# A second batch's preparation and end in another order, and the last expert tile of a MoE kept in SBUF

## The reference, cut to what matters

```python
def _rwkv7(r, k, v, xw, xa, xg, ...):            # 8 heads of 64
    logw = -softplus(-(w0 + tanh(xw) @ w_up)) - 0.5
    decay = exp(-exp(logw))
    a = sigmoid(a0 + xa @ a_up)
    kk = normalized(heads(k * k_k))
    k_mod = k * (1.0 + (a - 1.0) * k_a)
    y = _rwkv7_scan(r, decay, k_mod, v, kk, kk * a)
    yn = (y - mean(y)) * rsqrt(var(y) + GN_EPS) ...
    return (yn + bonus * v) * g

def hierarchical_moe(h, ...):                    # 16 experts, 2 per token
    weights, expert_idx = router(h)
    u = silu(hf @ w_gate[e]) * (hf @ w_up[e]) * combine
    return einsum("nef,efd->nd", u, w_down)
# afterwards: rmsnorm(x + moe, norm_final_g)
```

## Time and profile before

| | us |
|---|---|
| median of 3 runs (lowest to highest) | 1575.68 (1571.98 to 1575.98) |
| the profiled execution | 1576.64 |
| its span in the profile | 1574.4 |
| PE busy | 1473.1 (94%) |
| DVE, ACT, POOL busy | 739.1, 604.9, 464.0 |
| chain that ended last, PE's share | 83% |

### The profile page before, as it was taken

How to read it: one execution, slowest core, us unless ns; L and a number is a source line. 1 busy time by engine, 2 the same in 40 slices (tenths; PEclk the granted TensorE clock), 3 DMA queues, 4 the chain that set the end, 5 groups by cost and what they waited for, 6 DMA issues and landing times.

```text
span 1574.4 us, 19313 instructions
## 1 busy us (share of the span) xinstructions
PE 1473.1 (94%) x7736; PEld 1154.6 (73%) x7736; DVE 739.1 (47%) x1156; ACT 604.9 (38%) x948; POOL 464.0 (29%) x162
## 2 busy tenths in 40 slices
PE   6999997899879999999998999999999988699995
PEld 5878876688668888888876887666687867577762
DVE  3356277733353532515132596334352335566663
ACT  4443245322353332323134124533333444255552
POOL 2352122000225664646423444320134520200002
PEclk9999998657899999999998999999999999799998
DMA  6232112000135445354432333200123521889964
GB/s 209 87 121 68 56 66 95 2 1 1 46 129 160 135 146 159 124 158 142 139 107 80 98 112 99 80 27 27 49 85 107 188 58 67 346 314 422 419 261 188
DMA packets 97803, 203.90 MB, mean 130 GB/s; under 512 B 6672, under 2 KB 56208, under 8 KB 91056
## 3 DMA queue, kind: packets, MB, share of 16 engines
q1 hardware_dynamic: 90656, 176.94, 32.6%
q10 hardware_dynamic: 4752, 17.30, 2.7%
q0 software_dynamic: 2304, 8.39, 1.4%
HBM read 168.54 MB, written 34.08 MB: 129 GB/s over the span
## 4 chain that ended last, share of the span: by engine, by line
PE 83%; DVE 6%; ACT 5%; issue 3%; DMA 2%; POOL 1%; SPq 0%; POOLq 0%; DVEq 0%; ACTq 0%
PE bank L517 21%; PE bank L499 12%; PE bank L501 12%; PE bank L500 12%; PE bank L2770 4%; PE bank L780 3%; PE bank L799 3%; PE bank L790 2%; PE bank L1193 2%; PE bank L782 1%; ACT whi L428 1%; PE bank L706 1%; PE bank L2716 1%; PE bank L1149 1%; PE bank L1252 1%
## 5 line engine op out<-in xcount | busy, mean ns | idle before, releaser
L436 POOL TENSOR_TENSOR wlo<-raw,whi 128x2048 fp32r<-128x2048 f32 (+2 forms) x83 | 378.7, 4562 | 698.1 <-ACT whi L428 672.0
L428 ACT ACTIVATE whi<-raw 128x2048 fp32r<-128x2048 f32 (+1 forms) x84 | 159.1, 1894 | 279.6 <-PE bank L501 272.1
L517 PE MATMUL bank<-alo,whi 128*128 128x512 f32 x368 | 149.5, 406 | 4.9 <-DVE alo L728 4.9
L1986 DVE TENSOR_TENSOR ffn_relu<-ffn_relu 128x512 f32<-128x512 f32 x32 | 97.7, 3052 | 107.0 <-ACT ffn_relu L1966 107.0
L517 PE MATMUL bank<-ahi,whi 128*128 128x512 f32 x368 | 146.5, 398 | 0.0
L499 PE MATMUL bank<-alo,whi 128*128 128x512 f32 (+1 forms) x360 | 141.1, 392 | 0.0
L501 PE MATMUL bank<-ahi,wlo 128*128 128x512 f32 (+1 forms) x360 | 140.3, 390 | 0.0
L500 PE MATMUL bank<-ahi,whi 128*128 128x512 f32 (+1 forms) x360 | 140.1, 389 | 0.0
L517 PE MATMUL bank<-ahi,wlo 128*128 128x512 f32 x368 | 91.7, 391 | 0.0
L517 PEld LDWEIGHTS bank<-alo,whi 128*128 128x128 f32 x368 | 71.3, 194 | 23.5 <-DVE alo L728 6.1
L517 PEld LDWEIGHTS bank<-ahi,whi 128*128 128x128 f32 x368 | 71.4, 194 | 15.5 <-issue 0.7
(11 more groups left out here) (483 smaller groups left out, 3005.2 us busy)
## 6 DMA issues: line engine op xcount, KB each, us to landing
raw<-in_w_in_dram SPq DMA_DIRECT2D x18, 1024.0 KB, 5.1
expert_gate_up<-in_expert_w_gate_dram SPq DMA_DIRECT2D x17, 1024.0 KB, 11.8
expert_gate_up<-in_expert_w_up_dram SPq DMA_DIRECT2D x17, 1024.0 KB, 14.2
expert_down<-in_expert_w_down_dram SPq DMA_DIRECT2D x17, 1024.0 KB, 9.2
raw<-in_w_ffn_up_dram SPq DMA_DIRECT2D x16, 1024.0 KB, 6.2
raw<-in_w_ffn_down_dram SPq DMA_DIRECT2D x16, 1024.0 KB, 5.6
raw<-in_w_in_first_dram SPq DMA_DIRECT2D x12, 1024.0 KB, 5.5
expert_rows_dram<-zero_rows SPq DMA_DIRECT2D x23, 512.0 KB, 6.9
```

The costliest lines, as they stand in the source:

```text
L428: nc.scalar.activation(whi[:, n % SPLIT, 0:k * c], raw[:, n % RAW, 0:k * c], ACT.Copy).then_inc(hi_made, 1)
L436: nc.gpsimd.tensor_tensor(wlo[:, n % SPLIT, 0:k * c], raw[:, n % RAW, 0:k * c], whi[:, n % SPLIT, 0:k * c].bitcast(F32), ALU.subtract).the ...
L517: ins = nc.tensor.matmul(acc, of, by, start=first and i == 0, stop=last and i == products - 1)
L1986: nc.vector.tensor_tensor(relu2[:, n % 2, :], relu[:, n % 2, :], relu[:, n % 2, :], ALU.mult).then_inc(up_sq, 1)
```

## The change

Three places change. In the second batch, `FILL_LAST` is rewritten, rr1 and rv1/0 stay ahead of `over_norm` and rv1/1 comes behind it; `wlo` and `alo` move behind the preparation (`AFTER_PREP`); the product kk * aaa * e_inv is made as kk * (aaa * e_inv), so POOL needs e_inv and no longer kk; the end has another order. In the MoE, tile 16's result stays in SBUF and is added by PE with a selection matrix (`kept_w`, made from `kept_picks`), so that the gathers wait for tiles 14 and 15 only; down(15) stands ahead of the second half of gate_up(16); the order of the sums is changed. The branches for further tiles are nested, and their number is loaded early.

```diff
+        AFTER_PREP = 4
-        FILL_LAST = [0, 6, 6, 0, 3, 1, 1, 1, 1, 1, 1] + [1] * INVERT_PARTS + [2, 2, 2, 2, 2, 2, 2, 2, 2, 3, 3, 3, 3, 2, 2]
+        FILL_LAST = [0, 6, 3, 0, 3, 4, 1, 1, 1, 1, 1] + [1] * INVERT_PARTS + [2, 1, 1, 2, 2, 2, 2, 2, 1, 3, 3, 3, 2, 3, 5]
...
                 if made:
                     st.after("dve", made)
+                else:
+                    pe.wait_ge(z_shifted, 1 + [unit for unit, *_ in z_units].index(f"rv{p // 2}/{p % 2}"))
...
-            st.after("pool", "ka")
-            st.done(tt(b.beta[:, :], b.ka, b.e_inv, ALU.mult), "beta")
+            st.after("pool", "ae")
             st.after("dve", "kk")
+            st.done(tt(b.beta[:, :], b.kk, b.ae, ALU.mult), "beta")
...
         def pool_fill_last(pool):
-            yield from range(2 * WIDE_STEPS - 1)
+            yield from range(4 * WIDE_STEPS + AFTER_PREP)
             make_lo(pool, pool_slab, slab_no["rr1"] + 1 + SPLIT)
-            yield
-            yield from range(2 * WIDE_STEPS - 1)
             for p in (0, 1):
                 pool_rw_lo(pool, p)
             yield
...
-            st.after("dve", "kk")
-            st.done(tt(b.ka, b.kk, b.aaa, ALU.mult), "ka")
+            st.after("act", "e_inv")
+            st.done(tt(b.ae, b.aaa, b.e_inv, ALU.mult), "ae")
...
+        KEPT = SURE - 1
+        def tiles_beyond(eng, used, tile, i=SURE):
+
+            if i < MOE_TILES:
+                with eng.If(used > i - NE):
+                    tile(i)
+                    tiles_beyond(eng, used, tile, i + 1)
...
+            turn_hidden(pe, KEPT - 1)
+            pe_gate_up(pe, KEPT, 0)
+            pe_down(pe, KEPT - 1)
+            pe_gate_up(pe, KEPT, 1)
+            pe_sum_start(pe)
+            turn_hidden(pe, KEPT)
+            pe_down(pe, KEPT)
+            tiles_beyond(pe, used, lambda i: pe_later(pe, i))
             pe_sum(pe)
...
+            for t in SUM_ORDER:
...
+                nc.tensor.matmul(LEFT_BANKS[t][:, :], kept_w[:, t, :], y_rows[:, KEPT % 2, LEFT], start=t == IN_SBUF, stop=t == IN_SBUF,
+                                 skip_group_check=True)
+                nc.tensor.matmul(RIGHT_BANKS[t][:, :], kept_w[:, t, :], y_rows[:, KEPT % 2, RIGHT], start=True, stop=True).then_inc(halves_summed, 1)
...
+            in_order("rows rows kept rows kept rows kept final kept final final final",
+                     rows=dve_sum(dve, steps), kept=dve_sum_kept(dve, steps), final=dve_final(dve, steps))
...
-            for i in range(SURE - 2, SURE):
-                tile_done(pool, y_stored, i, 16)
+            for i in range(KEPT - 2, KEPT):
+                pool.wait_ge(*y_stored_at(i))
```

More of the change, by code:

```diff
@@ L886, in wk @@
                 return work[:, n:n + m, :].rearrange("p a n -> p (a n)")
-            b.cum, b.cumx, b.e_in, b.e_inv, b.e_ex, b.aaa, b.knorm, b.kk, b.kmod, b.ka, b.rk, b.sig = (wk(n) for n in range(12))
+            b.cum, b.cumx, b.e_in, b.e_inv, b.e_ex, b.aaa, b.knorm, b.kk, b.kmod, b.ae, b.rk, b.sig = (wk(n) for n in range(12))
             b.kr = put(f"rw_kr{s}", [P, NCH, 2, CHUNK])
@@ L1711, in pool_fill_last @@
             yield
-            yield from range(NHEAD * NT + 4 + TURN_ROUNDS - 1)
+            yield from range(NHEAD * NT + 4 + TURN_ROUNDS - 2 - AFTER_PREP)
             pool.wait_ge(rows_normed, turns["attn1"]["tile"] + NT)
@@ L2728, in pick_rows, with turn_kept_picks @@
                 ins.then_inc(rows_turned[0], 1)
+        def turn_kept_picks(pe):
+            pe.wait_ge(picks_made, 3 + 2 * NT + TOPK * NT)
+            for t in range(NT):
+                for k in range(TOPK):
+                    ins = nc.tensor.matmul(HIDDEN_BANKS[0][:, t * P:(t + 1) * P], kept_picks[:, k, t, :], ident,
+                                           start=k == 0, stop=k == TOPK - 1, skip_group_check=True)
+            ins.then_inc(halves_summed, 1)
         def pe_first_gate_up(pe):
@@ L2788, in pe_phase5 @@
             pe_first_gate_up(pe)
+            turn_kept_picks(pe)
+            used = later_tiles_used(pe)
             turn_rows(pe, 1)
-            for i in range(1, SURE):
+            for i in range(1, KEPT):
                 pe_gate_up(pe, i, 0)
+                if i == 1:
+                    pe.wait_ge(route_exps, 3)
                 turn_hidden(pe, i - 1)
@@ new lines, in pe_phase5, with pe_later @@
+            pe_gate_up(pe, KEPT, 0)
[5 more added lines that the diff above has]
+            tiles_beyond(pe, used, lambda i: pe_later(pe, i))
+            pe_sum(pe)
+        def pe_later(pe, i):
+            turn_rows(pe, i)
+            for c in range(CHUNKS):
+                pe_gate_up(pe, i, c)
+            turn_hidden(pe, i)
+            pe_down(pe, i)
+            tile_done(pe, y_left, i)
+            tile_done(pe, y_right, i)
+            pe_sum_start(pe)
@@ L2877, in act_phase5 @@
             act_tile_in(act, 3)
+            act.wait_ge(halves_summed, 1)
+            nc.scalar.activation(kept_w[:, :, :], four(HIDDEN_BANKS[0]), ACT.Copy).then_inc(route_exps, 1)
             for i in range(1, SURE):
@@ L3042, in dve_phase5 @@
                     steps.link(nc.vector.tensor_scalar(diag_w[:, k, t, :], ident, weight[:, k, t:t + 1], None, ALU.mult))
+            steps.link(nc.vector.tensor_scalar(kept_slot[:, :, :], slot_f[:, :, :], float(-KEPT * P), None, ALU.add))
+            for k in range(TOPK):
+                for t in range(NT):
+                    nc.vector.tensor_scalar(kept_picks[:, k, t, :], slot_no, kept_slot[:, k, t:t + 1], weight[:, k, t:t + 1],
+                                            ALU.is_equal, ALU.mult).then_inc(picks_made, 1)
             dve.wait_ge(rows_issued, 1)
@@ L3067, in dve_phase5, with dve_later @@
-            in_turn(dve_sum(dve), later(2, dve_final(dve, steps)))
-        def dve_sum(dve):
+            dve_y(dve, KEPT)
+            tiles_beyond(dve, used, lambda i: dve_later(dve, i))
+            in_order("rows rows kept rows kept rows kept final kept final final final",
+                     rows=dve_sum(dve, steps), kept=dve_sum_kept(dve, steps), final=dve_final(dve, steps))
+        def dve_later(dve, i):
+            for c in range(CHUNKS):
+                dve_w_lo(dve, i, c)
+            dve_x_lo(dve, i)
+            dve_hidden(dve, i)
+            dve_y(dve, i)
@@ L3078, in dve_sum, with dve_sum_kept @@
+        def dve_sum_kept(dve, steps):
+            for t in SUM_ORDER:
+                dve.wait_ge(halves_summed, KEPT_SUMMED[t])
+                if t == IN_SBUF:
+                    steps.link(nc.vector.tensor_tensor(x[:, t, LEFT], x[:, t, LEFT], LEFT_BANKS[t][:, :], ALU.add))
+                nc.vector.tensor_tensor(x[:, t, RIGHT], x[:, t, RIGHT], RIGHT_BANKS[t][:, :], ALU.add).then_inc(y_sums, 1)
                 yield
@@ L3163, in sp_phase5 @@
             sp_later(sp, NE)
-            for i in range(SURE, MOE_TILES):
-                with sp.If(used > i - NE):
-                    sp_later(sp, i)
+            tiles_beyond(sp, used, lambda i: sp_later(sp, i))
             out_view = out[0].rearrange("(t p) d -> p t d", p=P)
-            for t in range(NT):
-                sp.wait_ge(final_rows, 2 * t + 2)
+            for n, t in enumerate(SUM_ORDER):
+                sp.wait_ge(final_rows, 2 * n + 2)
                 sp.dma_start(out_view[:, t, :], out_rows[:, t, :]).then_inc(out_stored, 16)
```

168 lines of the change are left out of this document (91 added, 77 removed).

## The result

| | before | after |
|---|---|---|
| median, 20 runs each (us) | 1574.82 (1571.53 to 1578.58) | 1579.11 (1576.78 to 1582.56) |
| span of the profiled execution | 1574.4 | 1577.4 |

The ratio is 1.0027, 95% interval 1.0019 to 1.0034: the change makes the kernel 4.3 us slower. Forecast was 1573.0, some 3 us faster, with a range of 1563 to 1582. The time lies in the range, but the change goes the other way. The profiled executions differ by 3.0 us of span.

What follows compares the result with a forecast made beforehand. PE was taken to set the time, through its waits and clock. Preparation -1.2, middle and end +0.1, MoE -2.85 and +0.4 sum to -3.55 against the profiled 1576.64: 1573.1, taken as 1573.0; range 1563 to 1582.

Steps and rivals of the forecast that it cites:

- Bounds, and the order on POOL and DVE: Second batch's preparation: POOL's wlo starts first, the last kappa waits 4.6 us, PE restarts at 244.6 to 245.1.
- The preparation, -1.2: Second batch's preparation: 10.1 us from 244.9 give 255.0; -1.2 us with the earlier clock, bounds 0 and -8.5.
- The middle, -6.1 + 3.05 + 1.7: Two attention steps leave the low-clock stretch (-6.1), run later at full clock (+3.05); c2's wait and products inside attention (+1.7).
- The batch's end, +2.3 - 1.84 + 1.0: ACT's copies and squares ahead of splits (+2.3), var's products fill a wait (-1.84), opens may begin at low clock (+1.0).
- The MoE, -2.85 + 0.4: Gathers start 7.5 us earlier, DVE has 11.2 us behind the last (-2.85); small products at the front (+0.4).
- B: Preparation: DVE's last kappa starts before POOL's wlo, PE goes on near 239.9; 8.5 us gained, 1565; chance 0.22.
- C: Masks behind the preparation: the clock isn't back when they begin and may stay low; 12 us, 1585; chance 0.15.
- D: Middle, from 300 on: steady work releases the clock for a third of 70 us; 12 us gained, 1561; chance 0.05.
- E: No gain: the preparation's is lost to wlo and the MoE's to DVE; 1576; chance 0.13.

Runs made afterwards that it cites:

- bridged kernel: Kernel before plus 16 thrown-away products of the first tile's picks between its gate and up products and the second tile's turns: 1575.09 us, ratio 1.0004.
- old tail: Changed kernel with the last 15 numbers of FILL_LAST (from stage 15 on) as before: 1572.83 us, ratio 0.9987.
- prep_only: Kernel before with the preparation's part of the change alone, FILL_LAST from stage 15 on and second block as before: 1576.32 us, ratio 1.0007.
- late_two: Changed kernel, table moving two attention steps out of the low-clock stretch but leaving c2, c3, mean and var where they were before: 1569.25 us, ratio 0.9974.
- all_best: Changed kernel with the late_two table, POOL's wlo held back until kappa is done, and the last gathered left half summed by PE: 1562.37 us, ratio 0.9928.
- wlo_after_spread: Changed kernel, POOL's wlo at the batch's end waiting for DVE's spread of pair 3's deviations: 1575.59 us, ratio 1.0004.
- kappa_first: Changed kernel, POOL's wlo behind the preparation starting only after DVE's last kappa: 1577.80 us, ratio 1.0018.

## Why the prediction was wrong, by its own steps

**Bounds, and the order on POOL and DVE: right.** Khat at 232.3 (said 231.1), kappa of over 4 us from 239.87 (said near 238.5; the shift of khat by 6.6 us gives 238.0), PE's restart at 245.56 (said 244.6 to 245.1), the masks ahead by 0.5 us in the profile as it stands and 1.6 from the norm products (220.54 before, 221.65 after, the same instructions).

**The preparation, -1.2: wrong, it is no gain, about +1 (-0.3 to +2.7).** By its own numbers, 255.0 against 256.07, the forecast gain is 1.1. The step that failed is to take the kernel before as one whose clock comes back "some 9.4 us after the restart", a figure of one execution. From the norm products of stage 1 to the first mask the four profiles with the old order have 36.5, 33.9, 33.9 and 33.5 us; the execution that I worked from was the longest. The seven with the new order and the caught kappa have 34.7 to 35.9, mean 35.2, against a mean of 34.4. What differs is when the clock comes back, as the timeline of PE of the bridged kernel shows, whose first block is that of before:

```profile
249.48 0.72 PE L1185 MATMUL bank<-consts,zv 128*128 128x128 f32 x4
...
254.36 3.07 PE L1193 MATMUL bank<-rw_kr,rw_beta 64*128 64x256 f32 x13
```

It restarted at 246.65 and by 249.7 had the full clock. None of the seven with the new order has it before 254, 9.0 to 11.6 us after the restart. That is seen in eleven executions; why the new order doesn't meet the early return is not settled. From 300 to 360 PE loses another 0.4 to 0.9 us in the three kernels with the new preparation and the old tail (59.10 busy of 60 in `prep_only`, against 60.00 in the others); that attention being late is the cause isn't shown.

**The middle, -6.1 + 3.05 + 1.7: right.** From the first mask to the last scores of 512 keys, 257.07 to 387.54 before, 256.56 to 385.90 after: -1.1 us, where the three terms give -1.35. `late_two` tells them apart: 127.6 us there, 3.0 less than with the old tail for the two steps (said 3.05), and 1.7 less than in the changed kernel for the state (said 1.7). But the row of 393.25 is c1's and not c2's. c1 was moved ahead of the last scores, and c2 besides, with a wait of 0.77 and 1.48 us to the next products, ahead of the 14 products; the sum has no term for that.

**The batch's end, +2.3 - 1.84 + 1.0: the step that made the prediction wrong.** Middle and end together were put at +0.1 and measured +6.3. That the 16 small products of var "now fill a wait", -1.84, counted PE's share only. What comes behind them was not followed: the roots on ACT and the spread on DVE now stand ahead of the last split and the last alo, and POOL's wlo runs just then. From the last scores to the first open it is 31.0 us against 23.6, +7.4. With var back it is 26.8, so var's part is 4.3. With wlo behind the spread 1.7 of these go, the lock's share; the rest is the wait for var's products, 3.41 us at the low clock (1.84 before), for whose root the last ahi queues on ACT. The other 3.2 weren't taken apart by a run. By the timelines 2.0 lie ahead of c3 (400.36, against 399.96 for the state at this place before), of which the 14 products at the low clock are 1.5, and 1.1 behind it, where the mean's copies and squares stand on ACT (+2.3 said).


The lock between POOL and DVE was in my rows and I applied it to kappa alone. The Trainium skill, "SBUF — State Buffer", section "SBUF: two separate sides", says that the port pair which DVE and GpSimd share is an exclusive lock and is held for the whole instruction; both places agree, with 4.98 us against 0.68 once POOL's wlo was held back, and 3.50 against 0.43. The opens at the low clock cost 2.4 us and not 1.0, above the bound of 2: the first 24 passes take 8.04 us, 416.92 to 424.96, and took 5.60 before, 411.14 to 416.74.

**The low clock at the end.** This price was not in the sum. In all five profiles with c2 ahead of the last products of attention the clock falls before attention is through; in none of the nine others does it. So where the states stand decides it. By what mechanism is open. It suggests itself that PE's gaps there come together: it does 3.92 of 5 us from 385. But `all_best`, with c2 behind attention, has larger gaps and keeps the clock, by its windows:

```profile
380.00:385.00 5.00, 4.14 (x39) 3.12 (x38) 3.49 (x12) 2.33 (x7) 0.00 (x0) 1.00 0.00 0
385.00:390.00 5.00, 2.69 (x26) 2.48 (x22) 1.34 (x6) 2.33 (x4) 0.00 (x0) 1.00 0.00 0
```

Nor does it fall at a fixed place: in `wlo_after_spread`, the same order up to there, the last scores ran at the low clock and the 14 products at the full one (1.77 us).

**The MoE, -2.85 + 0.4 = -2.45: the sign right, the size too small.** Measured alone: -4.7 (-6.6 to -2.8). The term of the front is -1.7 and not +0.4 (-1.4 to -1.8 in all eleven profiles with this part): the products of the kept picks fill PE's wait, and the products behind them ran at 0.39 us in place of 0.63. At the end DVE is busy 11.2 us behind the last gather, as worked out; the first gather started 8.1 us earlier relative to the first down (7.5 said), but DVE began the last sums only 6.6 earlier, so the end gave 1.5 in place of 2.85. A slip in the bounds: DVE's 9 operations at up to 0.3 us make 2.7 and not 2.

**Rivals.** B (kappa isn't caught) didn't happen by itself; made to happen, it was worth 3.8 us ahead of the masks, not 7 to 8. C had the right sign with another place: not in the masks. D: from 300 to 360 the clock stays at 0.50 in every kernel, with PE busy for 59.10 us or more of 60. No rival had the batch's end; E came nearest.

Summed: MoE -4.7, preparation +1.1, tail +6.3 make +2.7; measured were 4.3, and the intervals of the parts (over 1 us to either side each) cover the rest.

## What to carry to other kernels

When a stage is moved, follow every engine's share of it to the instruction that is next in that engine's list, above all a DVE copy that will meet a long GpSimd operation. A gain ahead of a stretch in which the clock is at stake has to be measured with the rest of the order as it will be, since it can be given back there. Where TensorE waits between dense stretches (1.65 us here), work that is needed anyway can stand in that wait for nothing and keep the clock, worth 1.7 us here; work that is made up for it and is longer than the wait can cost as much as it gives.

## What was not expected of the hardware

After the same wait of some 7.8 us, on the same instructions, the clock came back between 3 us (bridged kernel) and 9.4 us (kernel before) after the restart, by the windows of the granted clock. So one profile fixes a term that depends on it no better than to 3 us. And with waits of only 1.35 and 1.21 us, 0.66 us of products between them, the clock fell in `kappa_first`.
